# Seven products instead of eight in the first gate/up pair, weight sums by an accumulating DMA, and an output stage with its sums one to three steps later

## The reference

```python
y = _rms(h, norm_ffn_g[i])
h = h + (jax.nn.silu(y @ w_gate[i]) * (y @ w_up[i])) @ w_down[i]   # D_FF = 5632
y = _rms(h, norm_ple_g[i])
h = h + jax.nn.sigmoid(y @ w_ple_gate[i]) * (p[i] @ w_ple_proj[i])
...
return (o * jax.nn.silu(gate)) @ w_out                               # second block
```

## Time and profile before

| | |
|---|---|
| median of 3 runs | 1395.29 us |
| the profiled execution's own time | 1396.01 us |
| its span in the trace | 1394.3 us |
| PE busy | 1385.0 us (99%) |
| DVE busy | 1146.4 us (82%) |
| ACT busy | 788.3 us (57%) |
| POOL busy | 79.5 us (6%) |
| granted TensorE clock | 1.00 |
| DMA | 318.32 MB, mean 228 GB/s |

### The profile page before, as it was taken

How to read it: one execution, slowest core, us unless ns; L and a number is a source line. 1 busy time by engine, 2 the same in 40 slices (tenths; PEclk the granted TensorE clock), 3 DMA queues, 4 the chain that set the end, 5 groups by cost and what they waited for, 6 DMA issues and landing times.

```text
span 1394.3 us, 16628 instructions
## 1 busy us (share of the span) xinstructions
PE 1385.0 (99%) x6239; PEld 1133.1 (81%) x6239; DVE 1146.4 (82%) x1355; ACT 788.3 (57%) x1074; POOL 79.5 (6%) x64
## 2 busy tenths in 40 slices
PE   9999999999999999999999999999999999999998
PEld 7888888888888888888888888888878887777886
DVE  6589976767999988999998889977677669887796
ACT  7476755554565544565555455555465556675453
POOL 2000010000000000000000000000000144420000
PEclk9999999999999999999999999999999999999999
DMA  9766656774775746675685655686877678889654
GB/s 334 246 208 212 206 169 204 257 245 133 263 247 191 234 170 224 232 243 194 212 269 185 226 211 196 212 296 208 284 249 278 220 260 258 268 260 298 193 187 151
DMA packets 171753, 318.32 MB, mean 228 GB/s; under 512 B 11953, under 2 KB 35757, under 8 KB 171544
## 3 DMA queue, kind: packets, MB, share of 16 engines
q1 hardware_dynamic: 156792, 285.37, 61.9%
q10 hardware_dynamic: 13088, 25.18, 5.8%
q0 software_dynamic: 1792, 6.71, 1.5%
HBM read 293.04 MB, written 24.17 MB: 228 GB/s over the span
## 4 chain that ended last, share of the span: by engine, by line
PE 90%; DVE 6%; DMA 2%; ACT 1%; issue 1%; SPq 0%; POOL 0%; ACTq 0%; DVEq 0%; POOLq 0%
PE acc L1924 15%; PE acc L1926 14%; PE acc L1925 14%; PE acc L2110 12%; PE acc L2113 12%; PE acc L2112 12%; DVE w_lo L1198 3%; PE acc L1986 1%; PE tp L2110 1%; PE tp L2113 1%; PE tp L2112 1%; PE sp L2113 1%; PE sp L2112 1%; PE sp L2110 1%; DMA parked<-tile 1%; PE sp L2214 1%
## 5 line engine op out<-in xcount | busy, mean ns | idle before, releaser
L795 ACT ACTIVATE w_hi<-w_raw 128x1024 fp32r<-128x1024 f32 x541 | 564.8, 1058 | 462.1 <-PE acc L1926 229.2
L1198 DVE TENSOR_TENSOR w_lo<-w_raw,w_hi 128x1024 fp32r<-128x1024 f32 x530 | 639.8, 1226 | 175.6 <-ACT w_hi L795 171.2
L1924 PE MATMUL acc<-w_lo,hh 128*128 128x512 f32 x528 | 207.9, 394 | 0.0
L1926 PE MATMUL acc<-w_hi,hl 128*128 128x512 f32 x528 | 205.7, 390 | 0.0
L1925 PE MATMUL acc<-w_hi,hh 128*128 128x512 f32 x528 | 205.6, 389 | 0.0
L2110 PE MATMUL acc<-w_lo,yh 128*128 128x512 f32 x460 | 179.7, 391 | 0.6 <-DVE w_lo L1198 0.6
L2112 PE MATMUL acc<-w_hi,yh 128*128 128x512 f32 x460 | 179.0, 389 | 0.0
L2113 PE MATMUL acc<-w_hi,yl 128*128 128x512 f32 x460 | 179.0, 389 | 0.0
L1924 PE MATMUL acc<-w_lo,yh 128*128 128x512 f32 x416 | 162.4, 390 | 1.1 <-DVE w_lo L1198 1.1
L1926 PE MATMUL acc<-w_hi,yl 128*128 128x512 f32 x416 | 161.9, 389 | 0.0
L1925 PE MATMUL acc<-w_hi,yh 128*128 128x512 f32 x416 | 161.9, 389 | 0.0
(11 more groups left out here) (277 smaller groups left out, 1756.1 us busy)
## 6 DMA issues: line engine op xcount, KB each, us to landing
w_raw<-in_w_gate SPq DMA_DIRECT2D x88, 512.0 KB, 5.5
w_raw<-in_w_up SPq DMA_DIRECT2D x88, 512.0 KB, 6.5
w_raw<-in_w_down SPq DMA_DIRECT2D x88, 512.0 KB, 5.9
...
```

The costliest lines, as they stand in the source:

```text
L795: act.activation(w_hi[:, v % SPL], w_raw[:, s % RAW], ACT.Copy).then_inc(hi_ready, 1)
L1198: dve.tensor_tensor(w_lo[:, v % SPL], w_raw[:, s % RAW], w_hi[:, v % SPL].bitcast(F32), ALU.subtract).then_inc(lo_ready, 1)
L1924: pe.matmul(dst, xh[:, f, tk], w_lo[:, v % SPL, k], start=(f == 0), stop=False)
L1926: last = pe.matmul(dst, xl[:, f, tk], w_hi[:, v % SPL, k], start=False, stop=(f == CK * n - 1))
```

## The change

1. The first pair gets three quads too (`FIRST_PLAN`, `FIRST_AT`; its functions `first_pair` on each engine are gone, and `pair(0)` runs it).
2. In pairs 0 to 10 the big sum is no longer DVE's: ACT copies the top halves of g and u into `wide` (`copy_tops`), POOL issues a DMA that adds the chunk u onto them in `wide`, and DVE forms the two remaining sums of 128x512 there (`sum_weights`, `last_sum`). The signs change with it. A table says before which split ACT copies (`copied`) and after which split DVE sums (`summed`). `PAIR_PLAN` has a new order.
3. Since `wide` is used for this, the projection is written to DRAM in the output projection of the first block (`put_proj`, four DMAs of 512 KB) and read back in the last down stage (`fetch_proj`).
4. In `PAIR_AT`, `hidden` moves from 2 to 1, `turn` from 5 or 7 to 2 or 5, `m1` to 12, `mix` mostly to 19, `gate` to 20.
5. In `SO_AT`, the splits of the last attention quarter move from 13 to 14, and `mix` and what follows by 1 (first block) or 2 (second block) steps.
6. The sums of the first pair's activations (`sum_y`) move into the output projection before it.

```diff
-PAIR_PLAN = plain(0, 3) + quad("g", 0) + plain(0, 4) + quad("u", 0) + plain(0, 5) + quad("t", 0) + quad("s", 0)
-PAIR_PLAN += plain(1, 3) + quad("g", 1) + quad("u", 1) + plain(0, 6, 7) + quad("g", 2) + quad("u", 2)
-PAIR_PLAN += quad("t", 1) + quad("s", 1) + quad("t", 2) + quad("s", 2) + plain(1, 4, 5, 6, 7)
+PAIR_PLAN = plain(0, 4, 3) + quad("g", 0) + plain(1, 4) + quad("g", 1) + quad("g", 2) + quad("u", 0) + quad("t", 0)
+PAIR_PLAN += quad("s", 0) + plain(1, 5) + quad("u", 1) + plain(0, 6, 5) + quad("t", 1) + quad("s", 1) + quad("u", 2)
+PAIR_PLAN += quad("t", 2) + quad("s", 2) + plain(0, 7) + plain(1, 7, 3, 6)
...
+SUMS = dict(copied={1: [0], 6: [1], 11: [2]}, summed={0: 5, 1: 11, 2: 15})
+FIRST_PLAN = plain(0, 3) + plain(1, 3) + quad("g", 0) + plain(0, 4) + quad("g", 1) + quad("g", 2) + quad("u", 0)
+FIRST_PLAN += quad("t", 0) + quad("s", 0) + plain(1, 4) + quad("u", 1) + plain(0, 5) + quad("t", 1) + quad("s", 1)
+FIRST_PLAN += quad("u", 2) + plain(0, 6) + quad("t", 2) + quad("s", 2) + plain(0, 7) + plain(1, 5, 6, 7)
+FIRST_AT = dict(low2=2, resid=2, turned=3, request=4, low3=12, m1=12, mix=20, gate=20, silu=21,
+                copied={1: [0], 5: [1], 10: [2]}, summed={0: 5, 1: 11, 2: 15})
-           2: dict(hidden=2, sums=4, turn=7, m1=19, mix=19, gate=19, low=21, silu=21, put=10, fetch=13),
-           3: dict(hidden=2, turn=7, m1=15, sums_high=17, mix=20, gate=20, sums_low=21, low=21, silu=21, put=10, fetch=13)}
+           2: dict(hidden=1, sums=4, turn=5, m1=12, mix=19, gate=20, low=21, silu=21, put=10, fetch=13, **SUMS),
+           3: dict(hidden=1, turn=2, m1=12, sums_high=17, mix=19, gate=20, sums_low=21, low=21, silu=21, put=9, fetch=12,
+                   **SUMS)}
...
-         dict(add=1, m1=11, mix=14, mixed_gate=15, mixed_up=16, bank=17)]
+         dict(add=1, m1=11, mix=16, mixed_gate=17, mixed_up=18, bank=19)]
@@ wait_raw_read: a slot is free when the DMA's quad is summed
             wait_low(eng, LAST_READ[s])
+            if s in LAST_SUM:
+                eng.wait_ge(w_sums, LAST_SUM[s])
@@ SyncE
+            def put_proj(j):
+                wait_left(sp_, PROJ_UNIT + j)
+                sp_.dma_start(proj(j)[1], proj(j)[0]).then_inc(proj_out, 16)
+            def fetch_proj(j):
+                wait_low(sp_, SPLITS.index(("s",) + BY_DMA[-1]))
+                sp_.dma_start(proj(j)[0], proj(j)[1]).then_inc(proj_in, 16)
-            for n, (i, c) in enumerate(WOVEN):
-                load(START[FFN_UNIT] + n, (wg_v, wu_v)[i], CK * c, 0)
-                if n in (4, 12):
-                    move(T_FFN + 2 + n // 8)
+            b = PAIR[0]
+            for i, p in enumerate(b.loads):
+                role = int(p[0] == "u" or p[:2] == ("n", 1))
+                load(b.raw + i, (wg_v, wu_v)[role], CK * p[-1], 0)
+                if i in (4, 12):
+                    move(T_FFN + 2 + i // 8)
@@ GpSimd
+            for i, (a, b) in enumerate(BY_DMA):
+                if i == 2:
+                    rsqrt(R_FFN, ms[:, R_FFN, 0:T], T, 1.0 / D)
+                pool.wait_ge(tops_copied, i + 1)
+                pool.dma_start(wide[:, i % 2, CW:3 * CW], w_raw[:, b % RAW].rearrange("p k n -> p (k n)"),
+                               accum_op=ALU.add).then_inc(tops_added[i % 2], 16)
@@ ScalarE
+            def copy_tops(b, q):
+                g, u = b.raw + b.loads.index(("g", q)), b.raw + b.loads.index(("u", q))
+                i = BY_DMA.index((g, u))
+                for s in (g, u):
+                    act.wait_ge(raw_in[s % RAW], 16 * (s // RAW + 1))
+                if i == 0:
+                    act.wait_ge(proj_out, 16 * NG)
+                if i >= 2:
+                    wait_low(act, SPLITS.index(("s",) + BY_DMA[i - 2]))
+                act.activation(weight_sums(g, u)[:, 1:3], w_raw[:, g % RAW:g % RAW + 2, 0],
+                               ACT.Copy).then_inc(tops_copied, 1)
@@ VectorE, split_low: after the split itself
+                if v - 1 in SUMMED_AT:
+                    last_sum(*SUMMED_AT[v - 1])
+                if v in SUMMED_AT:
                     wait_low(dve, v)
-                    sum_weights(a, b)
+                    sum_weights(*SUMMED_AT[v])
+            def sum_weights(a, b):
+                g, u, n = w_raw[:, a % RAW], w_raw[:, b % RAW], W_SUMS[a, b]
+                if (a, b) in BY_DMA:
+                    i, into = BY_DMA.index((a, b)), weight_sums(a, b)
+                    dve.wait_ge(tops_added[i % 2], 16 * (i // 2 + 1))
+                    dve.tensor_tensor(into[:, 3], u[:, 1], into[:, 1], ALU.add).then_inc(w_sums, 1)
+                    return
...
+            def last_sum(a, b):
+                g, u, n = w_raw[:, a % RAW], w_raw[:, b % RAW], W_SUMS[a, b]
+                dve.wait_ge(w_sums, n - 1)
+                if (a, b) in BY_DMA:
+                    into = weight_sums(a, b)
+                    dve.tensor_tensor(into[:, 0], g[:, 1], into[:, 3], ALU.add).then_inc(w_sums, 1)
@@ ScalarE, pair
+                    if i == b.at.get("low2"):
+                        ffn_turned_high(2)
+                    if i == b.at.get("low3"):
+                        ffn_turned_high(3)
```

More of the change, by code:

```diff
@@ L134 @@
             + quad("u", 1) + quad("s", 0) + plain(0, 6) + quad("t", 1) + quad("s", 1) + plain(1, 2, 3, 4, 5, 6, 7)]
-SO_AT = [dict(scale=2, turn=4, gated=12, low=13, m1=13, mix=16, mixed_gate=17, mixed_up=18, bank=19, put=10, fetch=10),
-         dict(add=1, m1=11, mix=14, mixed_gate=15, mixed_up=16, bank=17)]
-PAIR = {}
+SO_AT = [dict(scale=2, turn=4, gated=12, high=14, low=14, m1=13, mix=17, mixed_gate=18, mixed_up=19, bank=19, put=10, fetch=10),
+         dict(add=1, m1=11, mix=16, mixed_gate=17, mixed_up=18, bank=19)]
+PAIR = {0: Block(FFN_UNIT, FIRST_PLAN, **FIRST_AT)}
 for _m in range(1, PAIRS):
@@ L173 @@
         OWN[_b] = LAST_READ[_b] = _v
-    if _kind == "t":
+QUADS = sorted((_a, _b) for _kind, _a, _b in SPLITS if _kind == "u")
+W_SUMS = {}
+SUMMED_AT = {}
+BY_DMA = []
+_sums = 0
+for _block in BLOCKS:
+    if "summed" in _block.at:
+        BY_DMA += [(_block.raw + _block.loads.index(("g", _q)), _block.raw + _block.loads.index(("u", _q))) for _q in _block.quads]
+for _v, (_kind, _a, _b) in enumerate(SPLITS):
+    if _kind == "u" and (_a, _b) not in BY_DMA:
+        SUMMED_AT[_v] = (_a, _b)
+for _block in BLOCKS:
+    for _q, _i in _block.at.get("summed", {}).items():
+        SUMMED_AT[_block.v0 + _i] = (_block.raw + _block.loads.index(("g", _q)), _block.raw + _block.loads.index(("u", _q)))
+for _v in sorted(SUMMED_AT):
+    W_SUMS[SUMMED_AT[_v]] = _sums + (2 if SUMMED_AT[_v] in BY_DMA else 3)
+    _sums = W_SUMS[SUMMED_AT[_v]]
+for _v, (_kind, _a, _b) in enumerate(SPLITS):
+    if _kind == "t" and (_a, _b) not in BY_DMA:
         LAST_READ[_b] = _v
-    if _kind == "s":
+    if _kind == "s" and (_a, _b) not in BY_DMA:
         LAST_READ[_a] = _v
-QUADS = [(_a, _b) for _kind, _a, _b in SPLITS if _kind == "u"]
+LAST_SUM = {}
+for _a, _b in BY_DMA:
+    LAST_SUM[_a], LAST_SUM[_b] = W_SUMS[_a, _b], W_SUMS[_a, _b] - 1
 QUAD_BLOCKS = [b for b in BLOCKS if b.quads]
@@ L261, in build @@
     parked = nc.dram_tensor("parked", (P, 1024), F32, kind="Internal").ap()
+    parked_w = [nc.dram_tensor(f"parked_w{i}", (P, 1024), F32, kind="Internal").ap() for i in range(NG)]
     parked_m = [nc.dram_tensor(f"parked_m{i}", (P, 1024), F32, kind="Internal").ap() for i in range(3)]
@@ L409, in build @@
         w_sums = sem("w_sums")
+        proj_out = sem("proj_out")
+        proj_in = sem("proj_in")
+        tops_copied = sem("tops_copied")
+        tops_added = [sem(f"tops_added{i}") for i in range(2)]
         m1_copied = sem("m1_copied")
@@ L1035, in down @@
                         copy_m1(b)
-            first_pair()
-            for m in range(1, 4):
+            for m in range(4):
                 pair(m)
@@ L1165, in _ @@
                         og_high(2)
-                    if i == b.at.get("low"):
+                    if i == b.at.get("high"):
                         og_high(3)
@@ L1479, in _ @@
                         ffn_turned_low(j - 2)
+                    if j == 3 and c in (2, 5, 6, 7):
+                        for i in {2: (0,), 5: (1,), 6: (2,), 7: (3, 4)}[c]:
+                            sum_y(i)
             rf = rs[:, R_FFN]
-            def hidden_of_first():
-                wait_left(dve, FFN_UNIT)
-                wait_unit(dve, FFN_UNIT + 1)
-                for t in range(T):
-                    last = dve.scalar_tensor_tensor(tok(1)[:, t], acc[(FFN_UNIT + 1) % 2][t], rf[:, t:t + 1],
-                                                    tok(0)[:, t], ALU.mult, ALU.mult)
-                last.then_inc(left["d"], 1)
             def hidden(m):
-                if m == 0:
-                    hidden_of_first()
-                    return
                 b, up = PAIR[m], tok(1)
@@ L2084, in _ @@
                         to_features(H_OA, tok(5))
-            def first_pair():
-                for c in range(16):
```

(4 more changed lines are left out.)

192 lines of the change are left out of this document (97 added, 95 removed).

## The result

The changed kernel takes 1410.53 us (median of four executions, 1410.22 to 1413.1) against 1395.18 us for the kernel before (four executions too): a ratio of 1.0108, 95% interval 1.0093 to 1.0123. It is slower by 15.3 us; 1408.5 was predicted. The profiled execution is the longest of the four (1413.1, span 1411.4).

What follows compares the result with a forecast made beforehand. PE's matmuls were taken as the bound, DVE close behind. -2.04 - 1.86 + 9.3 + 2.4 + 7.5 - 1.45 - 0.6 = +13.25 us gave 1408.5 against 1395.29; 1402 to 1416 by its own bounds, stated range 1396 to 1424.

Steps and rivals of the forecast that it cites:

- Work of PE: First pair: with three quads PE has 9 matmuls fewer, -2.04 us.
- Waits that go: Pairs 2 and 6 and four block heads (pairs 3, 5, 7, 9): PE's late starts vanish as DVE is relieved, -1.86 us.
- The third quad: Pairs 1 to 10: a chain of splits and sums makes PE wait at s, 0.93 us per pair, +9.3 us.
- the ring of loads: Each pair: load 10 waits for quad 0's last sum, yet costs 0, or +0.5 us in pairs 2 and 6.
- Smaller holes: Pairs 3 and 7 (behind s2) and 2 and 6 (at t0): 0.6 us each, together +2.4, between 0 and 4.
- The first pair: First pair: two holes, 5.9 us at s1 and 1.6 us at s2, together +7.5 us.
- the large hole: First pair at s1: quarter 3's put and fetch come late behind three loads, so PE waits 5.9 us.
- The second (1.6): First pair at s2: the chain behind the first hole ends at 36.6, PE wants it at 35.2, 1.6 us.
- The output stage: Output stage: late starts at the second block's `mix` (-1.45 us) and first block's attention quarter (-0.6, 0.25 stays) go.
- The accumulating DMA: Pairs 1 to 10, third quad: POOL's DMA takes 6 us of 8.9 available, hidden; rival late sums, 10.5 us, chance 0.13.
- the start one DVE operation late: Each of the 33 POOL DMAs, by a skill rule, would start 1.2 us late, taken up by 2.9 us of slack.
- DVE's relief: DVE's busy time down by some 20 us: 30 sums of 1.225 gone, about 15 added in the first pair.

Runs made afterwards that it cites:

- the second try: The changed kernel with DVE's last sum of the third quad directly behind its first sum, before the low split of t: 1399.66 us (ratio 1.0022 to the kernel before).

## Why the prediction was right

It said +13.25 us and named the places; measured is +15.3 by the medians. The mechanism was right where most of the time went: the chain at the third quad, and the late quarter in the first pair. Point by point:

- *Work of PE*, -2.04: nine matmuls fewer, as counted.
- *Waits that go*, -1.86: the waits of the earlier trace rows are gone. Four of them stood elsewhere than the prediction says. The start at 414.24 is two plain chunks (5.4 us) before the end of pair 2, not at the head of pair 3, and its three likes are as far before the ends of pairs 4, 6 and 8. The sum is the same.
- *The third quad*, +9.3: ten holes, each step of the chain within 0.01 us in pair 1. Measured 10.3, since pairs 2 and 6 have 1.26 and 1.55. There ACT waited 1.5 and 3.3 us for a gate load (until 405.20 and 662.35 us), DVE's first sum came late and ACT's split of t began 0.32 and 0.61 late behind it. So this extra belongs to the ring of loads, which the prediction put at 0 to 0.5. That the hole itself is distance and not load is shown by the second try, which removes it with the same work on every engine.
- *Smaller holes*, +2.4: 0.51 in pairs 3 and 7, 0.32 in pairs 2 and 6, 1.7 together. Pair 6 has another 1.5, right behind ACT's wait of 3.3 us for the load.
- *The first pair*, +7.5: measured 9.2, made up otherwise. The way to the large hole was right: the put went out at 12.8 us (forecast 12.7) and ACT could take quarter 3 at 24.4 (forecast 23.8). The hole is 5.17 (forecast 5.9). One row was misread on the way, with little weight: the two loads of the earlier trace rows land 1.7 us apart and not 1.3, and the put landed 8.2 us after the first load of its burst (forecast 8.5). The second (1.6) does not appear, though it is real: it came back, at 1.58, when quarter 3 was early. In its place stand the slow matmuls (2.8), unforecast, which hid it, and the residual (1.24). I had DVE's residual over at 3.6 us (measured 3.8 after the pair's start at 293.30) and did not ask who waits for it: the accumulator of the second chunk. By itself it cost nothing, as the earlier residual shows, since it stood in front of the hole for quarter 3. That the total is near the forecast is in part luck: two terms that it did not have (4.0 together) stand against one that did not show (1.6) and one that was smaller (0.7).
- *The output stage*, -2.05: late starts 2.3 to 0.25, and exactly the 0.25 is left.
- *The accumulating DMA*: forecast 6 us against 8.9 us of room at the third quad. There the eleven took 5.0 to 8.6 (median 7.1), and in six of the pairs 1 to 10 the time from ACT's copy to the sum was 8.4; the longest of all, 9.0, belongs to a first quad with 10.9. The shortest of the 33, 4.5, is above the 3.2 that the prediction estimated by the fit, so that fit does not hold here. Hidden, but narrowly: in pairs 5 and 9 the result landed 0.1 us before the sum, and a copy two splits later cost 35 us. All 33 were issued 0.3 us after ACT's copy was over, in 0.86 to 0.97 us each, though DVE was at work at 31 of these moments. So the start one DVE operation late, which the prediction worked out, did not happen. It had stretched the rule: the Trainium skill (SBUF - State Buffer, the section on two separate sides) ties it to operations of DVE in a two-port mode and says that `tensor_tensor` has none, and at all 31 moments DVE ran a `tensor_tensor`. The trace agrees with that.
- *DVE's relief*: some 20 us forecast, 20.5 measured. What the DMA sums are worth I had not seen. I treated them as a saving on DVE, when the new order cannot do without them (40 and 51 to 54 us).

With the measured sizes the terms add to -2.04 - 1.86 + 10.3 + 1.7 + 1.5 + 9.2 - 2.05 = +16.7. The two profiled executions, 1396.01 and 1413.1, differ by 17.1. The rest lies where the prediction had no term. The first pair already begins 0.75 us later (293.30 against 292.55). A late start of 1.35 at 1015.37 us in the kernel before has no like in the kernel after, and 0.8 is lost in the attention before the output stage. With these the sum is 16.9. The profiles of the other changed kernels have such differences in some cases and not in others. By the medians the difference is 15.3; the profiled execution is 2.7 us above the other three of its kernel, and where that lies the trace of one execution can't say. So against the executions that the terms were read from the forecast is 3.8 us short, in the third quads (1.0), pair 6 (1.5) and the first pair (1.7) above all.
